# Weight sums of a seven-product matrix multiply: by additions, eight more chunks by seven, GpSimd's share to VectorE, and the second chunk loaded in halves

## The reference

```
first block, per layer:
  h += 0.5 * swiglu(rms_norm(h))                     # ffn1, 1024 -> 2 x 2816 -> 1024
  z_s, xbc, dt, qkv, z_d, b, a, gate_s, gate_d = rms_norm(h) @ w_in
  y_s = state space (conv and silu of xbc, chunked scan, times silu(z_s), norm)
  y_d = gated delta rule (conv and silu of qkv, chunked solve, norm, times silu(z_d))
  h += (sigmoid(gate_s) * (y_s @ wb_s) + sigmoid(gate_d) * (y_d @ wb_d)) @ w_out
  h += 0.5 * swiglu(rms_norm(h))                     # ffn2
second block, per layer:
  retention and convolution mixer; attention on a memory; ffn with a 3-tap convolution ("up", "down")
```

## Time and profile before

| | |
|---|---|
| median of 3 runs | 3204.95 us |
| the profiled execution, whole | 3207.67 us |
| its span on the core | 3205.9 us |
| TensorE busy (its weight loads) | 3187.9 us, 99% (3034.8 us) |
| VectorE busy | 2350.6 us, 73% |
| ScalarE, GpSimd busy | 665.5 us, 274.5 us |
| sums by VectorE, chunks | 343 |
| sums by GpSimd, chunks | 10 |

### The profile page before, as it was taken

How to read it: one execution, slowest core, us unless ns; L and a number is a source line. 1 busy time by engine, 2 the same in 40 slices (tenths; PEclk the granted TensorE clock), 3 DMA queues, 4 the chain that set the end, 5 groups by cost and what they waited for, 6 DMA issues and landing times.

```text
span 3205.9 us, 59487 instructions
## 1 busy us (share of the span) xinstructions
PE 3187.9 (99%) x25008; PEld 3034.8 (95%) x25008; DVE 2350.6 (73%) x5234; ACT 665.5 (21%) x1625; POOL 274.5 (9%) x339
## 2 busy tenths in 40 slices
PE   9999999999999999999999999999999999999998
PEld 9999999899999999998999999879999999889998
DVE  6657786276676577873867898877786988877885
ACT  1113433211111134332211111211211111212211
POOL 0202000001102020000011000300021000300031
PEclk9999999999999999999999999999999999999999
DMA  5544444344444444443544444344444445343453
GB/s 203 171 158 136 141 146 154 103 162 169 170 170 165 157 141 145 148 149 110 193 165 167 168 166 168 130 148 145 149 169 170 161 169 172 120 156 130 160 172 132
DMA packets 89643, 497.50 MB, mean 155 GB/s; under 512 B 25088, under 2 KB 29600, under 8 KB 30368
## 3 DMA queue, kind: packets, MB, share of 16 engines
q1 hardware_dynamic: 70608, 489.45, 44.8%
q10 hardware_dynamic: 18768, 4.25, 0.7%
HBM read 491.55 MB, written 2.11 MB: 154 GB/s over the span
## 4 chain that ended last, share of the span: by engine, by line
PE 94%; DVE 4%; ACT 1%; issue 0%; DMA 0%; ACTq 0%; DVEq 0%
PE bank L352 87%; DVE arena L1062 1%; DVE arena L1047 1%; DVE arena L1060 1%; PE bank L2063 1%; PE bank L2858 0%; PE bank L2117 0%; PE bank L2802 0%; PE bank L2839 0%; DVE arena L1059 0%; ACT arena L2425 0%; PE bank L2042 0%; DVE arena L2697 0%; DVE arena L2704 0%; PE bank L523 0%
## 5 line engine op out<-in xcount | busy, mean ns | idle before, releaser
L352 PE MATMUL bank<-arena 128*128 128x128 f32 x9240 | 1092.8, 275 | 2.6 <-DVE arena L1047 2.6
L352 PEld LDWEIGHTS bank<-arena 128*128 128x128 f32 x9240 | 1061.6, 192 | 3.4 <-DVE arena L1047 3.4
L352 PE MATMUL bank<-arena,ring 128*128 128x128 f32 (+1 forms) x6312 | 991.1, 310 | 2.4 <-DMA ring<-w 1.3
L352 PEld LDWEIGHTS bank<-arena,ring 128*128 128x128 f32 x6312 | 896.0, 192 | 59.6 <-issue 2.9
L352 PE MATMUL bank<-xT,ring 128*128 128x128 f32 (+1 forms) x5008 | 725.2, 300 | 0.3 <-DVE arena L1127 0.3
L352 PEld LDWEIGHTS bank<-xT,ring 128*128 128x128 f32 x5008 | 669.8, 192 | 31.0 <-issue 0.7
L1006 ACT ACTIVATE arena<-bank 128x128 f32<-128x128 f32 x311 | 85.9, 276 | 1105.3 <-PE bank L352 1099.5
L1059 DVE TENSOR_TENSOR arena<-ring 128x512 f32<-128x512 f32 x343 | 235.2, 686 | 107.1 <-PE bank L352 103.8
L1113 DVE TENSOR_TENSOR arena<-arena,bank 128x256 f32<-128x256 f32 x311 | 129.6, 417 | 220.0 <-ACT arena L1006 219.0
L352 PE MATMUL bank<-xT,arena 128*128 128x128 f32 x1928 | 255.6, 276 | 0.1
L1047 DVE TENSOR_TENSOR arena<-ring,arena 128x512 f32<-128x512 f32 x343 | 241.9, 705 | 11.5
(11 more groups left out here) (332 smaller groups left out, 2213.6 us busy)
## 6 DMA issues: line engine op xcount, KB each, us to landing
ring<-w SPq DMA_DIRECT2D x461, 1024.0 KB, 4.9
ring<-w SPq DMA_DIRECT2D x4, 256.0 KB, 5.6
hT<-hT_d ACTq DMA_DIRECT2D x4, 256.0 KB, 6.2
arena<-blocks_d ACTq DMA_DIRECT2D x4, 256.0 KB, 5.7
arena<-base_d ACTq DMA_DIRECT2D x16, 64.0 KB, 5.0
arena<-memT_d SPq DMA_DIRECT2D x1, 1024.0 KB, 9.1
outT<-hT SPq DMA_DIRECT2D x4, 256.0 KB, 2.5
arena<-dmask_d SPq DMA_DIRECT2D x1, 768.0 KB, 10.5
```

The lines of the kernel that those rows point to most:

```text
L352: ins = self.e.matmul(out, lhsT, rhs, start=start, stop=stop)
```

## The change

1. More chunks by seven in each layer of the first block: xbc 2, 4, 6, 8, 10, 11 (six for five), z_s 1 to 7 (seven for six), qkv 1, 2, 4, 5, 7, 8, 10, 11 (eight for six). That is four a layer, eight in all.
2. GpSimd makes no weight sums any more. VectorE makes those of xbc, inside its loop over n, the sums of chunk n+1 ahead of `join` and `conv` of chunk n.
3. The signs are turned so that two of the sums are additions with one common operand. They become one instruction of 128 x 1024; three instructions make the four sums. `join` needs four instructions for five. Output parts move between the two PSUM banks (X has three, Y four).
4. At the start chunk 1 is loaded in two halves, and TensorE begins on the first; on ScalarE's queue the first quarter of the input is issued ahead of the gain.

```diff
-BY_SEVEN = (2, 5, 6, 9, 10)
-Z_SEVEN = (1, 2, 3, 5, 6, 7)
-Q_SEVEN = (1, 3, 5, 7, 9, 11)
+BY_SEVEN = (2, 4, 6, 8, 10, 11)
+Z_SEVEN = (1, 2, 3, 4, 5, 6, 7)
+Q_SEVEN = (1, 2, 4, 5, 7, 8, 10, 11)
...
 def last_weights_by_dve(v, seven, ring, f):
-    e.tensor_tensor(s[:, 3, :], w[:, 1, :], s[:, 1, :], ALU.subtract).then_inc(sems.sum_by_dve, 1)
+    e.tensor_tensor(s[:, 3, :], w[:, 1, :], s[:, 2, :], ALU.add).then_inc(sems.sum_by_dve, 1)
 def weights_by_dve(v, seven, ring, f, last=True):
-    e.tensor_tensor(s[:, 0, :], w[:, 2, :], w[:, 3, :], ALU.add).then_inc(sems.sum_by_dve, 1)
-    e.tensor_tensor(s[:, 2, :], w[:, 0, :], w[:, 2, :], ALU.subtract).then_inc(sems.sum_by_dve, 1)
-    e.wait_ge(sems.sum_by_dve, 4 * SUMMED[f] + 1)
-    e.tensor_tensor(s[:, 1, :], s[:, 0, :], w[:, 0, :], ALU.subtract).then_inc(sems.sum_by_dve, 1)
+    e.tensor_tensor(s[:, 0:2, :], w[:, 2:3, :].to_broadcast([P, 2, GROUPS * P]), w[:, 0:4:3, :], ALU.add).then_inc(sems.sum_by_dve, 2)
+    e.wait_ge(sems.sum_by_dve, 4 * SUMMED[f] + 2)
+    e.tensor_tensor(s[:, 2, :], s[:, 1, :], w[:, 0, :], ALU.add).then_inc(sems.sum_by_dve, 1)
...
 def join(...):
+    e.tensor_tensor(quarter[:, 0:2, 0, :], twice(a), X[:, 1:3, :], ALU.add).then_inc(sems.bulk_read_dve, 1)
+    e.wait_ge(sems.bulk_done, BULK.filled(L, name, (i, 1)))
+    e.wait_ge(sems.bulk_read_dve, BULK.read(L, name, (i, 0)))
+    e.tensor_tensor(quarter[:, 0:2, 1, :], twice(u), Y[:, 1:3, :], ALU.subtract).then_inc(sems.dve_step, 1)
     e.wait_ge(sems.dve_step, seen.up("dve_step"))
+    e.tensor_tensor(last, Y[:, 0:2, :], twice(w), ALU.subtract).then_inc(sems.dve_step, 1)
+    e.tensor_tensor(quarter[:, 0, 1, :], quarter[:, 0, 1, :], Y[:, 3, :], ALU.add).then_inc(sems.bulk_read_dve, 1)
...
     for n in range(12):                                # first_dve, xbc
+        if n + 1 in BY_SEVEN:
+            weights_by_dve(v, m.seven_xbc, ring, FAST_FROM[L, "xbc_7"] + BY_SEVEN.index(n + 1))
         if n in BY_SEVEN:
...
 def first_pool(g, m, m2, L, cst, ring):
-    for i in range(len(BY_SEVEN)):
-        weights_by_pool(g, m.seven_xbc, ring, FAST_FROM[L, "xbc_7"] + i)
...
 def stream(e, sems, parts, ring, before):
+            if c == 1:
+                e.dma_start(ring[:, c, 0:SLOT // 2], dram[i][:, 0:SLOT // 2]).then_inc(sems.half_loaded, 16)
+                e.dma_start(ring[:, c, SLOT // 2:], dram[i][:, SLOT // 2:]).then_inc(sems.w_loaded[c], 16)
```

More of the change, by code:

```diff
@@ L394, in seven @@
         a = lambda i, g: self.whole[:, (i * GROUPS + g) * P:(i * GROUPS + g + 1) * P]
-        s = lambda i, g: sums.s[:, f % 2, i - 1, g * P:(g + 1) * P]
+        s = lambda i, g: sums.s[:, f % 2, SUM_OF[i], g * P:(g + 1) * P]
         part = lambda bank, i: bank[:, i * P:(i + 1) * P]
@@ L407, in summed @@
         def summed(n):
-            e.wait_ge(sems.sum_by_pool if f in BY_POOL else sems.sum_by_dve, 4 * SUMMED[f] + n)
+            e.wait_ge(sems.sum_by_dve, 4 * SUMMED[f] + n)
         def finished(ins):
@@ L417, in seven @@
             summed(4)
-            product(Y, 2, lambda g: s(4, g), "B22", first, False)
+            product(Y, 3, lambda g: s(4, g), "B22", first, False)
             if new:
                 product(Y, 1, lambda g: s(1, g), "T1", False, False)
-            product(X, 2, lambda g: s(2, g), "T2", False, False)
-            finished(product(X, 3, lambda g: s(3, g), "T3", False, last))
+            finished(product(X, 2, lambda g: s(2, g), "T2", False, last))
+            product(Y, 2, lambda g: s(3, g), "T3", False, False)
             if not new:
@@ L428, in seven @@
             summed(2)
-            product(X, 3, lambda g: s(3, g), "T3", False, False)
+            product(Y, 2, lambda g: s(3, g), "T3", False, False)
             summed(3)
@@ L433, in seven @@
             summed(4)
-            finished(product(Y, 2, lambda g: s(4, g), "B22", False, last))
+            finished(product(Y, 3, lambda g: s(4, g), "B22", False, last))
     def opening(self, outs, done, n, again=False):
@@ L453, in opening @@
                 e.wait_ge(sems.rows_loaded[k // 2], 16)
+            if n == 0 and again and (m, k) == (1, 0):
+                e.wait_ge(sems.w_loaded[1], 16)
             i = m * KD + k
@@ L706 @@
     multiply_fast(_L, "down", _at + CHUNKS2 - KF // 2, KF // 2, PAIRS, False)
-BY_POOL = {FAST_FROM[_L, "xbc_7"] + _i for _L in range(DEPTH) for _i in range(len(BY_SEVEN))}
-SUMMED = [sum((_g in BY_POOL) == (_f in BY_POOL) for _g in range(_f)) for _f in range(len(FAST))]
+SUMMED = list(range(len(FAST)))
 def feed(L, name):
@@ L1095, in sums_by_dve @@
     e.wait_ge(sems.tx_by_dve, at + 1)
[L1096 removed]
+    e.tensor_tensor(tx[1], tx[0], high[:, :, P:S], ALU.subtract).then_inc(sems.tx_by_dve, 1)
     e.wait_ge(sems.tx_by_dve, at + 2)
[L1098 to L1099 removed]
+    e.tensor_tensor(tx[2], low[:, :, P:S], high[:, :, P:S], ALU.subtract).then_inc(sems.tx_by_dve, 1)
+    e.tensor_tensor(tx[3], high[:, :, 0:P], tx[1], ALU.add).then_inc(sems.tx_by_dve, 1)
 def join(v, seven, L, name, i, high=None, in_place=False, to=None):
@@ L1209, in hidden @@
         e.wait_ge(sems.pool_step, g.seen.up("pool_step"))
-        e.tensor_tensor(th[2], high[:, P:S], low[:, P:S], ALU.subtract)
-        e.tensor_tensor(th[1], high[:, P:S], th[0], ALU.subtract).then_inc(sems.pool_step, 1)
+        e.tensor_tensor(th[2], low[:, P:S], high[:, P:S], ALU.subtract)
+        e.tensor_tensor(th[1], th[0], high[:, P:S], ALU.subtract).then_inc(sems.pool_step, 1)
         e.wait_ge(sems.pool_step, g.seen.up("pool_step"))
-        e.tensor_tensor(th[3], high[:, 0:P], th[1], ALU.subtract).then_inc(sems.th_ready, 1)
+        e.tensor_tensor(th[3], high[:, 0:P], th[1], ALU.add).then_inc(sems.th_ready, 1)
     for k in range(HALF):
@@ L1663, in first_dve @@
     for n in range(12):
+        if n + 1 in BY_SEVEN:
+            weights_by_dve(v, m.seven_xbc, ring, FAST_FROM[L, "xbc_7"] + BY_SEVEN.index(n + 1))
         if n in BY_SEVEN:
-            join(v, m.seven_xbc, L, "xbc_7", BY_SEVEN.index(n), in_place=True)
+            join(v, m.seven_xbc, L, "xbc_7", BY_SEVEN.index(n), in_place=True, to=m.pad[:, n % 2, :, 3:3 + S])
             if ROWS_AT <= n < ROWS_AT + 8:
```

35 lines of the change are left out of this document (9 added, 26 removed).

## The result

The changed kernel takes **3224.74 us** (median of 4 runs, 3224.09 to 3225.30), the kernel before 3205.55 (4 runs). The ratio is 1.0063 with a 95% interval of 1.0051 to 1.0074: slower by some 19 to 20 us, where the forecast was 3225.6. The profiled execution took 3224.09, its span 3222.3.

The account below looks back on a forecast made before the run. TensorE, busy for 99% of the span, was taken to bound the kernel. Terms of -5.3, +17.7, +4.2, +1.4, +3.4 and -0.8 summed to +20.6 us, giving 3225.6 us on the median; range 3216 to 3237.

Parts of the forecast that it names:

- eight chunks by seven: Eight more chunks at 6.25 us of TensorE instead of 6.91, each saving 0.66: -5.3 us.
- wait at chunk 2, two layers: In xbc, TensorE waits for VectorE's sums behind conv(0), 8.1 us in the first layer and 9.6 in the second: +17.7.
- low clock behind it: After chunk 2's wait TensorE's clock stays at half speed for a while: 2.1 us a layer, +4.2 in all, 0 to 6.8.
- end of xbc: Chunk 11 by seven puts three more join instructions ahead of conv(11), delaying TensorE 0.7 us a layer: +1.4.
- start: Chunk 1 loaded in halves shortens TensorE's first wait of 1.31 us: -0.8 us, 0 to -1.3.
- parts 1 to 3: Eight chunks by seven, -5.3 us; chunk 2's sums moved to VectorE, +17.7 and +4.2 for the clock; end of xbc, +1.4.
- part 4: Fewer instructions for sums and joins gain nothing; in "up" TensorE's waits grow 1.7 us a layer: +3.4, -2.6 to +5.
- So a chunk costs VectorE 0.11 us more, not less: In sums and joins: the merged sum costs 0.06 us more with its hand-over, the join 0.05 more.
- The rival that fewer instructions pay: In "up", shorter VectorE turns remove TensorE's waits, -2.6 us instead of +3.4; time 3219.6, chance 0.17.
- the main term: TensorE's wait at xbc's chunk 2 for sums moved from GpSimd to VectorE: +17.7 us over two layers.

Follow-up runs that it names:

- the second one of before: The kernel before, unchanged, profiled once more: 3204.30 us, span 3201.4.
- the run with one-column sums: Changed kernel, but GpSimd's sums in "up" are made of one column instead of 128: 3221.82 us, 1.0055 of the kernel before.
- The first run: Changed kernel, but the three sums of xbc's chunk 2 stand between the two openings, not behind conv(0): 3203.11 us, 0.9995 of the kernel before.
- the undo of part 2: Changed kernel, but GpSimd makes xbc's sums again, with the new signs: 3202.82 us, 0.9995 of the kernel before.
- with 9 and 11: Changed kernel, chunk 2's sums between the openings, later xbc sums two steps ahead, other chunks by seven, "up"'s last sum inside join: 3194.97 us.
- behind dt: Changed kernel, but chunk 2's sums stand behind dt's last step, ahead of conv(0): 3214.40 us, 1.0033 of the kernel before.
- the two runs with a pair of sums: Changed kernel, but two sums of 512 for the merged one: 3234.89 us; the same in the order of the kernel before: 3235.70 us.

## Why the prediction was right, and where it wasn't

What each term measured, as distances between the same TensorE instructions of the changed kernel's profile and of the second one of before:

| term | forecast | measured | how |
|---|---|---|---|
| eight chunks by seven | -5.3 | -5.2 | 8 steps of 0.65 or 0.66 |
| wait at chunk 2, two layers | +17.7 | +17.7 | 9.63 + 8.08 |
| low clock behind it | +4.2 | +5.3 | half of 5.07 and of 5.55 |
| low clock ahead of it, second layer | in no term | +1.7 | half of 3.42 |
| end of xbc | +1.4 | +1.5 | 2 x 0.75 |
| end of qkv | none | +0.5 | 2 x 0.27 |
| "up" | +3.4 | -0.5 | 2 x 0.26 |
| start | -0.8 | -0.6 | at the first layer's xbc |
| ends of the first block and of the kernel | none | +0.5 | 0.26 and 0.25 |
| sum | +20.6 | +20.9 | spans 3222.3 and 3201.4 |

**Right: parts 1 to 3.** The order on VectorE gave the wait to a tenth, since every step of it was in the trace of before: conv(0) hung on ScalarE's taps (2.23 us, as in the earlier trace rows), and the three sums took 1.25, 0.73 and 0.69 where 1.26, 0.72 and 0.69 were worked out. The merged sum is 1.22 like the row of the same size. That the two layers changed places (9.6 and 8.1 for 8.1 and 9.6) is the low clock ahead of chunk 2, which stood in the first layer of the one profile and in the second layer of the other. That each has it in one layer is chance: in the run with one-column sums neither layer has it, and both waits are 9.6. It takes from the wait nearly what it costs by itself, so the sum of the two terms moves little. The first run and the undo of part 2 show that the wait and its clock are the whole loss: without them 21.6 and 21.9 us go. The table's 17.7 + 5.3, less the new 2.4 at chunk 4, would be 20.6. The longer tail of xbc is join(11): with chunk 11 plain TensorE waits 0.28 there instead of 0.97.

```profile
327.05 1.23 PE L2029 MATMUL bank<-small 120*128 120x256 bf16 x6 [0.97 <-DVE arena L1687]
```

**Wrong: part 4, "up".** The step that failed is "So a chunk costs VectorE 0.11 us more, not less", taken for the early and the late half alike ("With 0.11 more per turn"). Neither half is so. Early, a turn went from 5.91 to 6.11, because the join costs 0.14 more, not 0.05: from its first to its second instruction, which waits for the first, it is 0.52.

```profile
2313.18 1.22 DVE L1068 TENSOR_TENSOR arena<-ring 128x1024 f32<-128x1024 f32 x1
2314.43 0.69 DVE L1070 TENSOR_TENSOR arena<-arena,ring 128x512 f32<-128x512 f32 x1
2315.16 0.69 DVE L1056 TENSOR_TENSOR arena<-ring,arena 128x512 f32<-128x512 f32 x1
2315.77 0.41 DVE L1104 TENSOR_TENSOR arena<-arena,bank 128x256 f32<-128x256 f32 x1
2316.29 0.42 DVE L1107 TENSOR_TENSOR arena<-arena,bank 128x256 f32<-128x256 f32 x1
...
2319.29 1.22 DVE L1068 TENSOR_TENSOR arena<-ring 128x1024 f32<-128x1024 f32 x1
```

Late, it went from 6.57 to 6.38. Before, beside GpSimd, the second and third sum took 0.94 each, and the four sums 3.19 from the first to join, the last row here:

```profile
2401.95 0.94 DVE L1060 TENSOR_TENSOR arena<-ring 128x512 f32<-128x512 f32 x1
2402.82 0.94 DVE L1062 TENSOR_TENSOR arena<-arena,ring 128x512 f32<-128x512 f32 x1
2403.79 0.83 DVE L1047 TENSOR_TENSOR arena<-ring,arena 128x512 f32<-128x512 f32 x1
2404.54 0.41 DVE L1113 TENSOR_TENSOR arena<-arena,bank 128x256 f32<-128x256 f32 x1
```

In the changed kernel GpSimd's step begins behind the merged sum, which keeps its 1.22, and the sums take 2.86:

```profile
2425.04 1.22 DVE L1068 TENSOR_TENSOR arena<-ring 128x1024 f32<-128x1024 f32 x1
2425.20 1.37 POOL L1195 TENSOR_TENSOR arena<-arena 128x128 f32<-128x128 f32 x1 [2.75 <-DVE arena L2691]
...
2426.29 0.83 DVE L1070 TENSOR_TENSOR arena<-arena,ring 128x512 f32<-128x512 f32 x1
...
2427.15 0.83 DVE L1056 TENSOR_TENSOR arena<-ring,arena 128x512 f32<-128x512 f32 x1
2427.90 0.41 DVE L1104 TENSOR_TENSOR arena<-arena,bank 128x256 f32<-128x256 f32 x1
...
2431.41 1.22 DVE L1068 TENSOR_TENSOR arena<-ring 128x1024 f32<-128x1024 f32 x1
```

VectorE makes up less early (0.14 a chunk for 0.34) and falls back less late (0.13 for 0.32), and TensorE's two waits at the end are 0.80 and 0.62 for 0.80 and 0.82. I had carried a cost from the rows without GpSimd to the rows beside it. The rival that fewer instructions pay named the right sign for the late half with the wrong reason: early, where no GpSimd works, the merged sum costs 0.05 more than the old pair, 1.25 for 1.20, as the term said.

**Mis-sized: the clock.** 2.1 a layer was taken from a dip of 3.3 us; behind the waits the low level lasted 5.1 and 5.6 us of work, a loss of 2.5 and 2.8, inside the range of 0 to 3.4.

**Unforeseen: the end of qkv.** Chunks 10 and 11 by seven, one after the other, end it 0.27 later a layer; with 9 and 11 it is 0.27 earlier again. The start can't be settled: the first norm's matmul stands at 14.2 in the changed kernel and 15.5 in the kernel before, but at 14.3 to 17.3 in the other kernels with the same split load.

So the total was right to a microsecond partly by luck: 3.9 too much in "up" stands against the clock's 2.8, qkv's 0.5 and the ends' 0.5 too little. The order behind the main term needed none. The medians are 19.2 apart and not 20.9; low stretches like the one of 1.7 needn't be in every run, but the other runs have no profile to show it.

## What to carry to other kernels

When work moves from an engine that had nothing else to do to one with a written order, its place in that order counts, not the load: look at when the consumer needs it and what stands ahead, and look for an idle gap further up. The same three instructions cost some 22 us behind conv(0) and 11 behind dt, by the medians against the run that has them between the openings, where TensorE didn't wait for them. A cost per turn read where one engine works alone doesn't hold where a neighbour works beside it; read it from the rows of that half.

## What the runs showed of the hardware

VectorE and GpSimd slow each other, and it is the one that begins second that takes longer. Of the changed kernel's 27 third sums (L1070) that began while a step of GpSimd ran, each took 0.82 or more; the other 334 took 0.69. The merged sum is no exception: where a step of GpSimd began during it, 24 times, it kept 1.22 and GpSimd's step, 0.45 to 0.46 alone, took 1.37. Three times it began second, and took 1.47 or more:

```profile
2440.87 0.78 POOL L1200 TENSOR_TENSOR arena<-arena 128x128 f32<-128x128 f32 x1
2441.26 1.47 DVE L1068 TENSOR_TENSOR arena<-ring 128x1024 f32<-128x1024 f32 x1
```

So in the late half merging pays because one instruction that begins first stands in the place of two, of which the second began beside GpSimd. Made of one column, GpSimd's step still took 1.10 and ended with the sum, 2406.98 for 2406.94; a step of one column that began as a sum ended took 0.18 (at 2407.66):

```profile
2405.72 1.22 DVE L1068 TENSOR_TENSOR arena<-ring 128x1024 f32<-128x1024 f32 x1
2405.88 1.10 POOL L1196 TENSOR_TENSOR arena<-arena 128x1 f32<-128x1 f32 x1 [3.55 <-DVE arena L2692]
2406.97 0.69 DVE L1070 TENSOR_TENSOR arena<-arena,ring 128x512 f32<-128x512 f32 x1
```

The Trainium skill ("Trainium Architecture — The Big Picture", "What this means for kernel authors") says that these two engines share a pair of ports under an exclusive lock, with no split of the bandwidth. This row agrees: GpSimd came second and ended with VectorE's sum.

A wait of 5 us left nearly as long a stretch of low clock behind it as one of 8 to 10 us, 4.5 to 5.0 us of work for 5.1 to 5.6, while the waits of about 1 us (at chunk 4, and those of "up" in the changed kernel's profile) left none. Between them, the waits of 3.0 us at the end of "up" in the two runs with a pair of sums left 3.4 us in three of four cases. In each such stretch the granted clock was 0.50, the lower of the two levels.
